# Two-layer hybrid encoder on one Trainium2 core: low parts of the first norm on VectorE, twelve modulation blocks computed during the first down-projection, and other filling products

## The reference, cut to what matters

```python
cs = silu(c)                                   # c: (1, 1024)
for i in range(2):
    mod = cs @ w_ada[i] + b_ada[i]             # w_ada: (2, 1024, 6144)
    shift1, scale1, gate1, shift2, scale2, gate2 = split(mod, 6)
    hm = rmsnorm(x, norm_g[i, 0]) * (1 + scale1) + shift1
    out = even_mixer(hm) if i == 0 else odd_mixer(hm)
    x = x + gate1 * rmsnorm(out, norm_g[i, 1])
    hf = rmsnorm(x, norm_g[i, 2]) * (1 + scale2) + shift2
    x = x + gate2 * rmsnorm(conv_glu(hf), norm_g[i, 3])
```

## Time and profile before

| | |
|---|---|
| median of 3 runs | 2977.65 us (2977.39 to 2981.0) |
| time of the profiled execution | 2982.81 us |
| its span | 2980.8 us |
| mean granted TensorE clock | 0.974 |
| TensorE (matmul) busy | 2874.6 us, 96% |
| VectorE busy | 1932.7 us, 65% |
| ScalarE busy | 1201.6 us, 40% |
| GpSimd busy | 455.9 us, 15% |

### The profile page before, as it was taken

How to read it: one execution, slowest core, us unless ns; L and a number is a source line. 1 busy time by engine, 2 the same in 40 slices (tenths; PEclk the granted TensorE clock), 3 DMA queues, 4 the chain that set the end, 5 groups by cost and what they waited for, 6 DMA issues and landing times.

```text
span 2980.8 us, 34629 instructions
## 1 busy us (share of the span) xinstructions
PE 2874.6 (96%) x13471; PEld 2275.2 (76%) x13471; DVE 1932.7 (65%) x2480; ACT 1201.6 (40%) x1937; POOL 455.9 (15%) x327
## 2 busy tenths in 40 slices
PE   7899999999999999999998999999799999999999
PEld 6667776766868888888866888878676788887887
DVE  6777866655488666654467767766726966666253
ACT  3123335713244333343345565555624433334252
POOL 1420011063002222221000000000000122222010
PEclk7999999999999999999999999999899999999999
DMA  6455466113433222265340111111123222225453
GB/s 212 150 183 168 143 201 220 48 57 126 142 102 103 83 80 85 85 224 154 116 153 15 35 42 46 52 42 42 64 92 106 78 85 85 84 72 182 146 156 116
DMA packets 361672, 326.62 MB, mean 110 GB/s; under 512 B 11485, under 2 KB 319166, under 8 KB 361470
## 3 DMA queue, kind: packets, MB, share of 16 engines
q1 hardware_dynamic: 348470, 271.61, 29.2%
q0 software_dynamic: 12000, 48.61, 4.3%
q10 hardware_dynamic: 1040, 4.19, 0.4%
HBM read 263.88 MB, written 68.35 MB: 111 GB/s over the span
## 4 chain that ended last, share of the span: by engine, by line
PE 89%; DVE 6%; ACT 2%; issue 1%; DMA 1%; POOL 0%; SPq 0%; ACTq 0%; DVEq 0%; POOLq 0%
PE psum_gemm L1870 20%; PE psum_misc L1870 18%; PE psum_gemm L2302 8%; PE psum_gemm L216 6%; PE psum_gemm L217 6%; PE psum_gemm L220 6%; PE psum_misc L2366 3%; PE psum_gemm L2387 3%; PE psum_gemm L2375 2%; PE psum_gemm L318 2%; PE psum_misc L216 2%; PE psum_misc L217 2%; PE psum_misc L220 2%; DVE ada_w L496 1%; PE psum_misc L866 1%
## 5 line engine op out<-in xcount | busy, mean ns | idle before, releaser
L216 PE MATMUL psum_gemm<-h_hi,w_hi 128*128 128x512 f32 x816 | 333.6, 409 | 18.5 <-POOL h_lo L403 7.8
L217 PE MATMUL psum_gemm<-h_lo,w_hi 128*128 128x512 f32 x816 | 322.0, 395 | 0.0
L1795 DVE TENSOR_TENSOR ring_lo<-piece_raw,ring_hi 128x512 fp32r<-128x512 f32 x192 | 138.0, 724 | 240.4 <-ACT ring_hi L1789 239.8
L198 ACT ACTIVATE w_hi<-w_raw 128x1024 fp32r<-128x1024 f32 x93 | 97.8, 1055 | 471.6 <-PE psum_gemm L220 339.3
L220 PE MATMUL psum_gemm<-h_hi,w_lo 128*128 128x512 f32 x816 | 254.4, 393 | 0.0
L203 DVE TENSOR_TENSOR w_lo<-w_raw,w_hi 128x1024 fp32r<-128x1024 f32 x93 | 122.5, 1321 | 142.6 <-ACT w_hi L198 142.6
L1789 ACT ACTIVATE ring_hi<-piece_raw 128x512 fp32r<-128x512 f32 x192 | 112.6, 592 | 241.7 <-PE psum_misc L1870 201.4
L216 PEld LDWEIGHTS psum_gemm<-h_hi,w_hi 128*128 128x128 f32 x816 | 155.2, 190 | 71.9 <-issue 32.6
L1870 PE MATMUL psum_misc<-h_hi,ring_hi 128*128 128x512 f32 x512 | 199.7, 390 | 0.2 <-DVE ring_lo L1795 0.2
L1870 PE MATMUL psum_misc<-h_hi,ring_lo 128*128 128x512 f32 x512 | 199.2, 389 | 0.0
L1870 PE MATMUL psum_misc<-h_lo,ring_hi 128*128 128x512 f32 x512 | 199.2, 389 | 0.0
(11 more groups left out here) (408 smaller groups left out, 6853.7 us busy)
## 6 DMA issues: line engine op xcount, KB each, us to landing
ada_w<-in_w_ada SPq DMA_DIRECT2D x40, 1024.0 KB, 5.3
w_raw<-in_f_w_up SPq DMA_DIRECT2D x52, 512.0 KB, 4.5
ffn_act_scratch<-gate_act SPq DMA_DIRECT2D x42, 512.0 KB, 2.6
piece_raw<-in_f_w_down SPq DMA_DIRECT2D x80, 256.0 KB, 2.9
piece_raw<-ffn_act_scratch SPq DMA_DIRECT2D x80, 256.0 KB, 2.9
pair_raw<-in_f_w_up SPq DMA_DIRECT2D x36, 512.0 KB, 4.9
w_raw<-in_e_w_in SPq DMA_DIRECT2D x29, 512.0 KB, 6.5
x_scratch<-x_res SPq DMA_DIRECT2D x3, 4096.0 KB, 12.5
```

The costliest lines, as they stand in the source:

```text
L198: act.activation(w_hi[:, s], w_raw[:, s], ACT.Copy).then_inc(s_hi, 1)
L216: pe.matmul(o, wh, rh[:, k, c], start=(k == 0), stop=False)
L217: pe.matmul(o, wh, rl[:, k, c], start=False, stop=False)
L1795: dve.tensor_tensor(Al[:, idx % 7, 0:n], src, Ah[:, idx % 7, 0:n].bitcast(F32), ALU.subtract).then_inc(s_wl, 1)
```

## The change

The low parts of the first norm are all made by VectorE, each behind the next tile's scaling, as in the later norms; ScalarE no longer writes the shifted value back. Between the last modulation block of setup and the first product of unit 0, TensorE makes four float32 products of 512 columns on x. The units 1 and 2 have no modulation block now, the units 3 to 8 one each, the units 9 to 20 ten as before, the units 21 to 25 two and the units 26 and 27 one each. The blocks 36 to 47 are made in the down-projection of layer 0: VectorE's steps at the pieces `LATE`, SyncE's load four pieces earlier, TensorE's product four pieces later, in memory that holds x's tiles 4 to 7. So x comes back in two parts, tiles 0 to 3 at m = 9 and tiles 4 to 7 at m = 84, and the twelve rows are turned at m = 88. `residual(2)` has twelve filling products ahead of the sums in place of eight, and none on the first weights.

```diff
-ADA_START, ADA_XS, ADA_Z, ADA_END = 8, 24, 34, 48
+ADA_START, ADA_XS, ADA_Z, ADA_END, ADA_ALL = 8, 14, 24, 36, 48
...
-        LO_POOL = 5
+        LO_POOL = 0
...
-                keep_clock_pe(eng, e, 8)
+                keep_clock_pe(eng, e, 12 if e == 2 else 8)
...
-                    for _ in range(2):
-                        eng.matmul((pM if e == 2 else pG)[:, 1, HALF:], w_f[:, 0, 0:P], w_f[:, 0, 0:HALF], start=True, stop=True)
+                    for _ in range(0 if e == 2 else 2):
+                        eng.matmul(pG[:, 1, HALF:], w_f[:, 0, 0:P], w_f[:, 0, 0:HALF], start=True, stop=True)
...
                 between(eng)
+                if e == 0:
+                    eng.wait_ge(s_fc, 4)
+                    for _ in range(4):
+                        eng.matmul(pG[:, 1, HALF:], X[:, 0, 0:P], X[:, 0, 0:HALF], start=True, stop=True)
...
             if u < U_XS:
-                return [ADA_START + 2 * (u - U_U), ADA_START + 2 * (u - U_U) + 1]
+                return [ADA_START + u - U_U - 2] if u >= U_U + 2 else []
...
-            return [ADA_Z + 2 * (u - U_Z), ADA_Z + 2 * (u - U_Z) + 1] if u < U_OUTB - 1 else []
+            if u - U_Z < 5:
+                return [ADA_Z + 2 * (u - U_Z), ADA_Z + 2 * (u - U_Z) + 1]
+            return [ADA_Z + 10 + u - U_Z - 5] if u < U_OUTB - 1 else []
...
-                    sp.dma_start(X[:], x_dram.rearrange("k p s -> p k s")).then_inc(s_xf, 16)
+                    n = KT if L else 4
+                    sp.dma_start(X[:, 0:n], x_dram[0:n].rearrange("k p s -> p k s")).then_inc(s_xf, 16)
+                m = x - RING_UP
+                for n, step in enumerate(LATE):
+                    if not L and m == step - 4:
+                        late_load(sp, ADA_END + n)
+                if not L and m == LATE_END:
+                    ge(sp, s_red, ADA_ALL + 1)
+                    sp.dma_start(X[:, 4:KT], x_dram[4:KT].rearrange("k p s -> p k s")).then_inc(s_xf, 16)
...
+        LATE = [14, 18, 22, 26, 30, 52, 56, 60, 64, 68, 72, 76]
+        LATE_END = LATE[-1] + 8
...
+        def late_load(sp, b):
+            if b < ADA_END + 2:
+                ge(sp, s_pp, 7 * 17 + 3)
+            else:
+                ge(sp, s_red, b)
+            l, c = divmod(b * 256, 6 * D)
+            sp.dma_start(ada_wl[:, b % 2], unit_src(io["w_ada"][l], 0, 8, c, 256)).then_inc(s_late[b % 2], 16)
...
+                if not L and m - 4 in LATE:
+                    ada_pe(pe, ADA_END + LATE.index(m - 4))
+                if not L and m == LATE_END + 4:
+                    late_turn_pe(pe)
...
+                if not L and m in LATE:
+                    ada_dve(dve, ADA_END + LATE.index(m))
+                if not L and m == LATE_END:
+                    late_copy_dve(dve)
+                if not L and m == LATE_END + 5:
+                    late_mods_dve(dve)
```

More of the change, by code:

```diff
@@ L413, in norm @@
                     eng.wait_ge(s_t1, KT * e + k + 1)
-                    if not np:
+                    if e:
                         eng.wait_ge(s_pair, KT * (e // 2 - 1) + k + 1)
@@ L470, in ada_src @@
         def ada_src(eng, b):
+            if b >= ADA_END:
+                ge(eng, s_late[b % 2], 16 * ((b - ADA_END) // 2 + 1))
+                return ada_wl[:, b % 2]
             if b < ADA_START:
@@ L490, in ada_dve @@
                     dve.wait_ge(s_avc, n + k)
-                if k == KT - 1 and b >= ADA_START + 2:
+                if k == KT - 1 and ADA_START + 2 <= b < ADA_END:
                     dve.wait_ge(s_red, b - 1)
@@ L502, in ada_pe @@
             pe.wait_ge(*ada_owner(b))
+            if b >= ADA_END:
+                r = b - ADA_END
+                pe.matmul(pG[0:NR, 0, 512:768], pick[:, NR - 1 - r:2 * NR - 1 - r], ada_part(b), start=(r == 0),
+                          stop=(b == ADA_ALL - 1), skip_group_check=True).then_inc(s_red, 1)
+                return
             if b >= ADA_START:
@@ L1097, in mods_dve, with shift_splits @@
             for m in range(2):
-                dve.tensor_tensor(mods[:, 16:96].rearrange("p (r m) -> p r m", m=2)[:, :, m], pM[:, 1, m * NR:(m + 1) * NR],
-                                  par[:, 0, 16:96].rearrange("p (r m) -> p r m", m=2)[:, :, m], ALU.add).then_inc(s_mods, 1)
+                dve.tensor_tensor(mods[:, 16:16 + 2 * NR].rearrange("p (r m) -> p r m", m=2)[:, :, m], pM[:, 1, m * NR:(m + 1) * NR],
+                                  par[:, 0, 16:16 + 2 * NR].rearrange("p (r m) -> p r m", m=2)[:, :, m], ALU.add).then_inc(s_mods, 1)
             dve.wait_ge(s_mods, 4)
-            for l in range(2):
-                for h in range(2):
-                    if (l, h) != (0, 0):
-                        scale_coef(dve, l, h)
-                    gate_coef(dve, l, h)
+            for l, h in ((0, 0), (0, 1), (1, 0)):
+                if (l, h) != (0, 0):
+                    scale_coef(dve, l, h)
+                gate_coef(dve, l, h)
+            shift_splits(dve, (0, 1), 8)
+        def shift_splits(dve, ns, done):
             def shift(n):
@@ L1109, in shift, with late_copy_dve, late_turn_pe, late_mods_dve @@
                 return mods[:, o:o + 8]
-            for n in range(len(SHIFTS)):
+            for n in ns:
                 dve.tensor_copy(bhl[:, n, :, 0], shift(n)).then_inc(s_small, 1)
-            dve.wait_ge(s_small, 8 + len(SHIFTS))
-            for n in range(len(SHIFTS)):
+            dve.wait_ge(s_small, done)
+            for n in ns:
                 dve.tensor_tensor(bhl[:, n, :, 1], shift(n), bhl[:, n, :, 0].bitcast(F32), ALU.subtract).then_inc(s_small, 1)
+        NL = ADA_ALL - ADA_END
+        LATE = [14, 18, 22, 26, 30, 52, 56, 60, 64, 68, 72, 76]
+        LATE_END = LATE[-1] + 8
+        LATE_SMALL = AT_FIRST[0] + 3 + 3
+        def late_load(sp, b):
[5 more added lines that the diff above has]
+            sp.dma_start(ada_wl[:, b % 2], unit_src(io["w_ada"][l], 0, 8, c, 256)).then_inc(s_late[b % 2], 16)
+        def late_copy_dve(dve):
+            dve.wait_ge(s_red, ADA_ALL + 1)
+            dve.tensor_copy(ada_rl[0:NL, :], pG[0:NL, 0, 512:768]).then_inc(s_mods, 1)
+        def late_turn_pe(pe):
+            pe.wait_ge(s_mods, 5)
+            for m in range(2):
+                mm = pe.transpose(pG[:, 0, 768 + m * NL:768 + (m + 1) * NL], ada_rl[0:NL, m * P:(m + 1) * P],
+                                  ident[0:NL, 0:NL])
+            mm.then_inc(s_red, 1)
+        def late_mods_dve(dve):
+            dve.wait_ge(s_red, ADA_ALL + 2)
+            c = slice(2 * ADA_END, 2 * ADA_ALL)
+            for m in range(2):
+                dve.tensor_tensor(mods[:, c].rearrange("p (r m) -> p r m", m=2)[:, :, m],
+                                  pG[:, 0, 768 + m * NL:768 + (m + 1) * NL],
+                                  par[:, 0, c].rearrange("p (r m) -> p r m", m=2)[:, :, m], ALU.add).then_inc(s_mods, 1)
+            dve.wait_ge(s_mods, 7)
+            scale_coef(dve, 1, 1)
+            gate_coef(dve, 1, 1)
+            shift_splits(dve, (2,), LATE_SMALL)
         xS = at("x_S", 0, [P, CH, 1024])
@@ L1738, in build @@
         ss = at("row_squares", MS + 4, [P, 8])
+        ada_wl = at("ada_w_late", 16, [P, 2, 8, 256])
+        ada_rl = at("ada_rows_late", MS + 4.25, [P, 256])
+        s_late = s_evin
         s_gev, s_vev = sem("gate_evacuated"), sem("value_evacuated")
@@ L1749, in build @@
                                        (s_s1, 4), (s_c11, 8), (s_tr, 7), (s_tlV, 7), (s_rlV, 7), (s_dev, 7), (s_ps, 7),
[L1750 to L1751 removed]
+                                       (s_tlO, 7), (s_rlP, 14), (s_t3, 20), (s_as, 32), (s_par, 176), (s_atl, 96), *((s, 224) for s in s_gl),
+                                       (s_late[0], 15), (s_late[1], 14), *((s, 16) for s in (*s_pl, *s_xin)))}
         def ge(eng, s, n):
@@ L1830, in x_turn @@
             if n == 0:
-                ge(pe, s_xf, 64)
+                ge(pe, s_xf, 80)
                 ge(pe, s_c11, 2 * PAIRS)
@@ L1936, in ffn_pe @@
                     gate_row_pe(pe)
+                if not L and m - 4 == LATE[0]:
+                    ge(pe, s_c11, PAIRS)
+                    ge(pe, s_cb, 5 * PAIRS)
+                if not L and m - 4 in LATE:
+                    ada_pe(pe, ADA_END + LATE.index(m - 4))
+                if not L and m == LATE_END + 4:
+                    late_turn_pe(pe)
         def ffn_early_act(act, u0):
```

20 lines of the change are left out of this document (9 added, 11 removed).

## The result

The changed kernel takes 2959.84 us (median of 4 runs, 2954.95 to 2964.82), the kernel before 2979.1 us, measured beside it (4 runs): ratio 0.9942, 95% interval 0.9925 to 0.9960, faster by 0.6%. The forecast was 2956, from 2949 to 2966. In three further groups of runs the kernel before had medians of 2976.72 to 2980.19, and the unaltered changed kernel, in two of them, 2959.66 and 2960.04. The gain is thus 17 to 19 us where the sum said 21.8. The forecast that the kernel gets faster, and by about how much, was right. But all four terms of the sum were off: the first two gains came out too small and the cost in the down-projection too large, while the last gain was larger than forecast. That the number fits all the same is in part luck, as the account at the end shows.

What follows compares the result with a forecast made beforehand. TensorE was taken to bound the kernel (89% of the chain). The terms -4.1 - 17.7 + 0.4 + 0.6 - 1.0 = -21.8 us took 2982.81 to 2961.0; corrected by 5.2 to the median, 2956, range 2949 to 2966.

Steps and rivals of the forecast that it cites:

- (c): Units 2 to 9: much loss from pooling's copy and addition chain; gain 8 to 11, total 2963 to 2966; chance 0.07.
- (d): Down-projection: VectorE's dependent steps starve the ring throughout; 2.8 us a block, 34 in all, total 2990; chance 0.03.
- (e): Whole kernel: no change in time, the gain being spent elsewhere; chance 0.03.
- (a): Down-projection: late blocks stall the ring around m = 48 to 56; +5 to +8 us, total 2961 to 2964; chance 0.13.
- (b): Clock falls in the first norm, unit 5 and `residual(2)`; 2.4 us each, total 2959 to 2963; chance 0.17.
- signs of being wrong: Clock low again between 100 and 140 us, or TensorE waiting for `ring_lo` after the resident tiles.
- Part 1: First norm: unit 1 ends at 89.6, 4.1 us earlier, the fillings delaying nothing; bounds -1.7 to -5.
- Part 2: Units 2 to 9: idle 4.0 us instead of 14.9, at full clock; gain 17.7 us, bounds 10.9 to 19.
- so I take the full clock: Units 2 to 9: no wait over 2 us, so no clock loss; lost 4.0 us instead of 21.7.
- Part 3: Down-projection's twelve blocks: `ada_pe` only moves (0), +0.4 for second turn and units 26, 27, +0.6 at m = 48 to 56.
- the ring has three pieces (8 us) in hand: Down-projection at m = 52: the ring's lead covers the block's 4.1 us; +0.6 us taken, bounds 0 and 8.
- Part 4: `residual(2)`: without the two float32 fillings `unnormed_pe` begins earlier; -1.0 us, -2.7 if the clock stays up, +2.4 if it falls.

Runs made afterwards that it cites:

- Both edits: Changed kernel with late blocks at pieces 14 to 34 and 60 to 80, and unit 9's block after `pool_g`: 2954.5 us, then 2952.48 side by side.
- the steps apart: Changed kernel with two late blocks moved from m = 52 and 56 to 34 and 80, loads and products too: 2953.8 us, then 2954.65 side by side.
- the changed kernel again: The changed kernel rerun unaltered, as base of the first group: 2959.66 us, ratio 0.9942 to the kernel before.

## Why the prediction was right, and which terms were off

Its direction was right for its reasons, its number in part by luck. The main steps held: TensorE bounds the kernel, the modulation blocks on VectorE cause the waits and most falls of the clock in units 2 to 9, and the down-projection takes the blocks without a general shortage of VectorE (rivals (c), (d) and (e) are out: the blocks bring 12 us, the pure price in the new place is 10.3). Rivals (a) and (b) both came true in part: a stall behind the resident tiles, and a fall of the clock in one of the three places that (b) names, `residual(2)`, beside one in unit 9, which it doesn't name. Of the signs of being wrong one came: TensorE waited for `ring_lo` after the resident tiles, 1.13 us in this execution and 0.18 before. The terms one by one:

**Part 1, -4.1, measured -3.1.** The pace and the pattern came as written (2.39 us a tile, 1.28 a subtraction; the fillings took 5.47 us, less than the 5.9 to 6.9 of the estimate, and don't delay the third tile). Scaling began at 62.50 and not at 61.96, so the third tile came at 71.11, not 70.5; that is 0.6 of the missing 1.0. The other 0.4 was not traced. The experiments part the gain: all but 0.65 us of it is due to the subtractions' move.

**Part 2, -17.7, measured -13.9** (21.8 less the 7.9 of the ten blocks). The three waits that were followed are all there, each longer than taken: 1.6 for 1.2 after unit 2, 1.7 for 0.9 in unit 5, 2.7 for 1.9 in unit 9, 6.0 for 4.0 in all. For the first, a slip stands in the working: 2, four times 2.05 and 1.5 are 11.7 us and not 12.1, so its own terms give 0.8. The step that failed beside this is "so I take the full clock": after the wait of 2.7 us the granted clock was 0.57 over 4 us, which is 1.7 us lost. 2.0 and 1.7 make the 3.8 that are missing. The reason for taking it was a wait of 1.9 us that had left the clock at 1.00; one of 2.7 at the same place is not that case. Both edits of the experiment above bring the unit's end to the forecast's place by removing this wait.

**Part 3, 0 + 0.4 + 0.6.** The mis-sized term is the "+0.6" at m = 48 to 56. Over six profiles with the steps at m = 52 (the changed kernel three times, and the three experiments that change the first norm or `residual(2)`) the stretch took 648.2 to 654.3 us, in the mean 650.5; in four with the steps apart 645.8 to 647.0, in the mean 646.4. The tight place thus costs 4.1 us, and up to 8 in one execution. The sentence that was wrong is "the ring has three pieces (8 us) in hand". It does have three, pieces 57 to 59; but 58 and 59 are short, so they are 5.4 us. More than that, the block's own product stands ahead of them in TensorE's queue. VectorE made the low part of piece 59 at 1403.35 and began the block at 1403.69; TensorE had ended piece 56 by 1403.8 and asked for the block at once. Against this wait the lead is nothing, whatever the ring holds. In the ordinary places the same order is harmless: there ScalarE and VectorE wait for TensorE to free the slot of piece m before they make piece m + 7, so a block begun at m has until piece m + 4 is done, 10.9 us. At m = 52 they come when 56 is done. This is read from the timelines and the code. What the runs show is that the cost goes when loads, steps and products leave this place together. How it is shared is not shown: with the product alone queued later, the one profile has most of it gone (647.2 us), with the loads alone issued earlier as well (647.4 us), and in neither case do the times tell. The late landing of piece 59, for which VectorE waited before it began the block, is thus the rival of the product's place in the queue, and each may have a part.

**Part 4, -1.0, measured -2.4** against before, and +2.2 when it is undone. It went the upper way that the prediction bounded with -2.7: with the longer filling the clock stayed up through the sums, the turns and the second pair of `shift_pe` halves (1.03 us each, not 1.84 as in the earlier trace rows). The large products on `h_unnormed` begin 12.41 us after the mark before the stretch, where it was 15.16: 2.75 earlier, of which 0.3 is lost again. What was mis-sized is the choice of -1.0 for a case that came in ten of twelve profiles. The two float32 products are not what the gain hangs on: in the experiment that put them back, TensorE waited behind them. The clock still falls, at the large products, after 2.22 us of idle time. By the rule of the Trainium skill (TensorE: Matmul & The Clock Gate, the section on the clock gate) that the throttled state is the default and activity releases it, read as in the prediction, this would have been a loss of 2.4 us; the fall did come under the large products, as that reading has it, but the stretch ahead of it gave back more.

**The clock elsewhere.** The terms as measured in this pair of profiles (-3.1, -13.9, +18.0 - 9.5 = +8.5, and -2.4) give -10.9, where the spans differ by 17.8. The 6.5 us of the last stretch make up for most of the rest, and as far as the runs can tell they are chance: with the same instructions as before, the kernel with the blocks back in their place took 1419.4 us there, the profile of before 1428.9. The profile on which the sum stands was a long one in that stretch. The sum was corrected by the 5.2 us between its time and the median; without that correction it would have said 2961.0. With the down-projection at its mean of six profiles the terms give -3.1 - 13.9 + 4.7 - 2.4 = -14.7, and the medians 17 to 19. So the sum was 7 us too large, and the 2 to 5 us that the terms leave unexplained brought the time near it: that is the luck in the number, and its cause stays open.

## What to carry to other kernels

When work is moved into a stage with a ring, count the lead against the moved work's own consumer and its place in the queue, not against the ring, and count it in the real lengths of the pieces that lie between. Where the ring has just run empty and the helping engines wait for pieces to land, it has no lead (here 3.9 us of idle time), so put the moved steps before that place or well after it. Price an edit by a mark just behind it in the profile; a gain of 2 us is plain there, and four to six executions of a program of 3000 us did not show it. Look at the mark in more than one profile, since the clock moves it too.

## What the runs showed of the chip that was not expected

The same instructions take a different time from one profile to the next, by whether the clock falls. The stretch around `residual(2)` took 93.06 to 93.12 us in ten profiles with the new filling, and 97.4 and 94.3 in two more with the same instructions there; one of these two and one of the ten are executions of the same kernel. Behind the resident tiles, a wait of 2.5 us for the block left the granted clock at 1.00 (the low parts back on GpSimd), while one of 2.2 was followed by a fall (the changed kernel again). The last stretch took 1419.4 to 1424.9 us over thirteen profiles.

The wait of 2.7 us before unit 9's `pool_product` is another case. It was followed by a fall in all eight profiles of kernels with the steps at m = 52, and by none in the two profiles of the kernel with the steps apart, whose instructions are the same up to there. So this fall went with the kernel and not with the execution, and no run shows why.

A fall of the clock behind one wait of 1 to 4 us is thus nothing to take as given, with or without. In these two places, without the wait there was none; in `residual(2)` it also came after 0.36 us of idle time. Single executions of the changed kernel went from 2954.95 to 2964.82, while its three medians, of four to six executions each, lie within 0.4 us, and the four of the kernel before within 3.5.
